# Blocked expert matmuls of a transformer layer pair: the loads of the down matrices issued by another engine

## What is computed

```python
def hierarchical_moe(h, rg_w, rg_b, re_w, re_b, w_gate, w_up, w_down):
    ...
    xs = xt[slot_tok].reshape(n_blocks, MOE_BLOCK, D)

    def expert_block(args):
        xb, e = args
        a = xb @ w_gate[e]
        u = xb @ w_up[e]
        return (jax.nn.silu(a) * u) @ w_down[e]

    ys = lax.map(expert_block, (xs, block_expert)).reshape(n_slots, D)
    ys = ys * slot_gate[:, None].astype(ys.dtype)
    out = jnp.zeros((T, D), ys.dtype).at[slot_tok].add(ys)
```

## Time and profile before

| | us |
|---|---|
| Median of 3 runs | 2011.5 |
| Lowest and highest | 2010.38, 2014.53 |
| The profiled execution's own time | 2010.09 |
| Its span, first to last instruction | 2008.8 |
| TensorE busy | 1814.8 |
| VectorE, ScalarE, GpSimd busy | 846.3, 437.2, 982.7 |
| Moved on q1 (SP), q10 (ScalarE), q0 (GpSimd) | 315.12, 19.46, 10.78 MB |

### The profile page before, as it was taken

The page is one execution under the profiler, slowest core; times in us unless marked ns, Lnnn a source line. Parts: engine busy times, 40 slices in busy tenths (PEclk is TensorE's granted clock), DMA queues, the critical chain, the costliest instruction groups (busy, mean ns, idle before and its releaser), DMA issues.

```text
span 2008.8 us, 27496 instructions
## 1 busy us (share of the span) xinstructions
PE 1814.8 (90%) x9716; PEld 1274.7 (63%) x9716; DVE 846.3 (42%) x1248; ACT 437.2 (22%) x813; POOL 982.7 (49%) x532
## 2 busy tenths in 40 slices
PE   8999999999999899999999889998968978969783
PEld 6888888887676678888888656765733333323231
DVE  6444433310444577444444489876341111111114
ACT  3111100100344432111100144552421111111112
POOL 6888887777444378888887533321211111101001
PEclk9999999999999999999999989999979989979887
DMA  4333372433111133333333212210588999999995
GB/s 160 94 96 102 106 267 88 145 94 94 53 57 50 43 89 91 101 95 94 94 112 100 73 53 73 66 54 28 235 312 325 401 403 399 401 415 412 411 393 207
DMA packets 56977, 346.00 MB, mean 172 GB/s; under 512 B 8474, under 2 KB 8858, under 8 KB 44896
## 3 DMA queue, kind: packets, MB, share of 16 engines
q1 hardware_dynamic: 44640, 315.12, 43.0%
q10 hardware_dynamic: 7968, 19.46, 2.6%
q0 software_dynamic: 4320, 10.78, 1.6%
HBM read 475.06 MB, written 19.66 MB: 246 GB/s over the span
## 4 chain that ended last, share of the span: by engine, by line
PE 71%; DMA 14%; DVE 10%; ACT 3%; issue 1%; POOL 1%; SPq 0%; DVEq 0%; ACTq 0%; POOLq 0%
PE bank L471 31%; PE bank L442 12%; DMA big<-w_up_in 11%; PE bank L1850 7%; PE bank L723 4%; PE bank L1349 4%; PE bank L1868 2%; DVE big L1075 2%; PE bank L490 2%; PE bank L1463 2%; DMA ring<-w_down_in 1%; PE bank L1876 1%; PE bank L641 1%; DVE state L1060 1%; PE bank L701 1%
## 5 line engine op out<-in xcount | busy, mean ns | idle before, releaser
L282 POOL TENSOR_TENSOR weights_hi_parts<-ring,ones 128x1024 fp32r<-128x1024 f32 (+1 forms) x174 | 351.4, 2019 | 291.9 <-PE bank L471 127.7
L284 POOL TENSOR_TENSOR ring_parts<-ring,weights_hi_parts 128x1024 fp32r<-128x1024 f32 (+1 forms) x174 | 468.7, 2693 | 13.6
L471 PE MATMUL bank<-attention_buffers_parts,weights_hi_parts 128*128 128x512 f32 x832 | 325.6, 391 | 11.4 <-DVE ring_parts L510 10.0
L471 PE MATMUL bank<-state_parts,weights_hi_parts 128*128 128x512 f32 x832 | 324.4, 390 | 0.0
L471 PE MATMUL bank<-attention_buffers_parts,ring_parts 128*128 128x512 f32 x832 | 324.2, 390 | 0.0
L1850 PE MATMUL bank<-big,work 128*32 128x512 f32 x1440 | 227.5, 674 | 51.3 <-DMA big<-w_up_in 51.1
L442 PE MATMUL bank<-big_parts,weights_hi_parts 128*128 128x512 f32 x704 | 216.8, 389 | 1.2 <-POOL ring_parts L284 1.2
L1950 POOL TENSOR_TENSOR small<-small 128x1 f32<-128x1 f32 x51 | 9.6, 189 | 375.0 <-DVE small L1773 375.0
L895 POOL TENSOR_TENSOR ring_parts<-ring,weights_hi_parts 128x1024 fp32r<-128x1024 f32 x32 | 80.6, 2520 | 222.6 <-ACT weights_hi_parts L892 222.6
L471 PEld LDWEIGHTS bank<-attention_buffers_parts,weights_hi_parts 128*128 128x128 f32 x832 | 156.6, 188 | 44.8 <-issue 10.5
L471 PEld LDWEIGHTS bank<-state_parts,weights_hi_parts 128*128 128x128 f32 x832 | 156.6, 188 | 33.0 <-issue 0.5
(11 more groups left out here) (391 smaller groups left out, 2833.6 us busy)
## 6 DMA issues: line engine op xcount, KB each, us to landing
big<-w_up_in SPq DMA_DIRECT2D x54, 2048.0 KB
ring<-wdense_in SPq DMA_DIRECT2D x176, 512.0 KB, 3.5
state<-w_down_in SPq DMA_DIRECT2D x37, 2048.0 KB
big<-w_gate_in SPq DMA_DIRECT2D x36, 2048.0 KB
attention_buffers<-w_gate_in SPq DMA_DIRECT2D x18, 2048.0 KB
ring<-w_down_in SPq DMA_DIRECT2D x18, 2048.0 KB
ring<-wff_in SPq DMA_DIRECT2D x32, 704.0 KB, 4.1
y_rows<-big ACTq DMA_DIRECT2D x1, 8192.0 KB, 28.0
```

The lines of the kernel that those rows point to most:

```text
L282: po.tensor_tensor(hi, raw, ones[:, 0:1].to_broadcast([128, words]), ALU.mult).then_inc(PO.sem, 1)
L284: po.tensor_tensor(lo, raw, hi.bitcast(F32), ALU.subtract) \
L471: m = pe.matmul(out, x, y_, start=j + n == 0, stop=j == len(pairs) - 1 and n == len(ts) - 1)
```

## The change

All down loads of the loop are issued by ScalarE, on its own queue. In ScalarE's loop `load_down` stands behind the silu and ahead of the stores of the previous block, and loads for block c + 2 while c is worked on. It waits for the same step of TensorE as before. SP's loop keeps the gate and up loads alone. The skipped load for block 2 is gone, and with it the 16 in the third set's wait. Ahead of its first block ScalarE waits for the tables.

```diff
-    def load_expert(m, b, e, needed=None):
+    def load_expert(m, b, e, needed=None, eng=sp):
 
         if needed is None:
-            d = sp.dma_start(sets[b][m], experts_d[m][e])
+            d = eng.dma_start(sets[b][m], experts_d[m][e])
         else:
-            d = sp.dma_start(sets[b][m], experts_d[m][bass.ds(e, 1), :, :].rearrange("a p c -> p (a c)"), cond=needed)
+            d = eng.dma_start(sets[b][m], experts_d[m][bass.ds(e, 1), :, :].rearrange("a p c -> p (a c)"), cond=needed)
         d.then_inc(s_wexp[m][b], 16)
...
-        pe.wait_ge(s_wexp[2][b], i * 16 + (16 * (c // SETS) + (32 if b == 2 else 16)))
+        pe.wait_ge(s_wexp[2][b], i * 16 + (16 * (c // SETS) + 16))
...
     def load_down(i, c):
 
-        e = sp.value_load(exp_i[0:1, bass.ds(i * SETS + c, 1)].bitcast(I32), min_val=0, max_val=N_EXP - 1)
-        needed = sp.value_load(need[0:1, bass.ds(i * SETS + c, 1)].bitcast(I32), min_val=0, max_val=1)
-        sp.wait_ge(PE.sem, at_step(PE, PE_D, i, c - SETS + 1))
-        load_expert(2, c % SETS, e, needed)
+        e = ac.value_load(exp_i[0:1, bass.ds(i * SETS + c, 1)].bitcast(I32), min_val=0, max_val=N_EXP - 1)
+        needed = ac.value_load(need[0:1, bass.ds(i * SETS + c, 1)].bitcast(I32), min_val=0, max_val=1)
+        ac.wait_ge(PE.sem, at_step(PE, PE_D, i, c - SETS + 1))
+        load_expert(2, c % SETS, e, needed, ac)
...
     with sp.Fori(0, laps["sp"]) as i:
         for c in range(SETS, 2 * SETS):
             load_first(i, c)
-            load_down(i, c - 1)
-    load_down(laps["sp"], SETS - 1)
...
+    ac.wait_ge(DV.sem, tables.base)
     act_copy(0, 0)
     act_silu(0, 0, 2)
     with ac.Fori(0, laps["ac"]) as i:
...
             act_copy(i, c)
             act_odd(i, c - 1)
             act_silu(i, c)
+            load_down(i, c + SETS - 1)
             act_store(i, c - 1)
```

## The result

| | before | changed |
|---|---|---|
| Median, us | 2012.15 (4 runs) | 2060.28 (4 runs) |
| Lowest and highest | 2010.38, 2014.53 | 2059.64, 2063.5 |
| The profiled execution, span | 2010.09, 2008.8 | 2060.82, 2059.6 |

The ratio is 1.0239, with a 95% interval of 1.0225 to 1.0254. The change costs 48.1 us; 55.8 were forecast, with a range of 2040 to 2084. A fourth run of the kernel before moved its median from 2011.5 to 2012.15.

The account below looks back on a forecast made before the run. The prediction took the DMA engines, busy share 1.00 over 413 us, to bound the block loop. Its terms, 9 + 30.8 + 5 + 11 = 55.8 us, gave a median of 2067 us from 2011.5, range 2040 to 2084.

Parts of the forecast that it names:

- Start of the loop: Loop start: down loads 3 and 4 share the engines with gate and up loads, delaying gate/up 5; cost 9 us.
- Four gaps: After up loads 14, 20, 26 and 38: engines idle through gate/up until the next gate load; 7.7 us each, 30.8.
- the one that I had called the weakest: In each burst of loads: all down loads overtake the burst's last up load; the gaps rest on it.
- one of the forecast's signs of being wrong: End of the loop: the forecast is wrong if block 50's down load still lands after its up load.
- Short gaps: Behind up loads 23, 29, 35, 47: ScalarE issues some 2 us later, engines wait; 5 us, between 0 and 8.
- The 31.6 in its upper bound: Four-gap share of the range's upper end: 10.5 + 31.6 + 8 + 11 + 10, 71 us above 2011.5.
- Order at the end: End of the loop: down loads 49 and 50 served ahead of up load 50, 11.0 us later; 5.5 if only one.
- Down waits: TensorE's waits for down matrices in the loop: 4.0 us go, but nothing is counted as gained.
- ScalarE: zero forecast: ScalarE between silu and next copy: some 1.9 us more work just fits in 3.32; zero cost, 10 us without cover.
- no change: Rival for the queues: ScalarE's gets engines only when SP's is empty, or bytes alone decide; 2011 us, chance 0.04.
- The half case: Rival for the bursts: one down load of each pair stays behind the up load; 20 us, 2032, chance 0.10.
- The bound on ScalarE: Rival in undisturbed blocks: issuing takes ScalarE 1 us or more, making copies late; 18 us on top, 2085, chance 0.08.

Follow-up runs that it names:

- the second profile of the changed kernel: The changed kernel run once more unaltered, on the chip of the two kernels that moved half of the down loads: 2059.0 us, ratio 1.0223.
- the two split kernels: Changed kernel with only part of the down loads on ScalarE, the rest on SP: buffer sets 0 and 1, 2035.9 us; set 2 alone, 2034.3 us.
- the one with 4 KB pieces: Changed kernel with the down matrices laid out in HBM so that down loads move in 4 KB pieces, not 16 KB: 2022.8 us, ratio 1.0065.
- the control: Kernel before, all loads on SP's queue, with down loads in 4 KB pieces: 2014.9 us, ratio 1.0014.
- the one with the swap on SP: Kernel before with the down load of block n-1 issued ahead of block n's gate and up loads on SP's queue: 2055.7 us, ratio 1.0233.
- the reads alone: Kernel before with ScalarE also reading each down load's two registers behind its silu, issuing no loads: 2014.6 us, ratio 1.0016.

## Why the prediction held, step by step

The direction, the mechanism and the range were right; the number was 7 us high. In part that is luck: the terms are all about the loop, which took 46.2 us more for 55.8 forecast, and 4.5 us ahead of the loop, in no term, made up for some of the miss. Gate/up 14, 20, 26, 38 and 50 start 16.1, 23.2, 29.6, 39.5 and 47.5 us later against the loop's start; about 19, 26, 35, 46 and 55 were forecast. By its terms, from the start times of gate/up 5, 50 and 53 counted from gate/up 0:

1. Start of the loop: 9 forecast. Gate/up 5 comes 54.8 us after gate/up 0 where it came after 46.5: 8.3.
2. Four gaps: 7.7 us each, 30.8, forecast. Measured from load to load 5.6, 7.9, 4.9 and 5.2: 23.6. This is the term that was mis-sized, and the step behind it is that all down loads of a burst overtake its last up load, the one that I had called the weakest. They nearly do. D14 is issued at 1601.40; counted from the loop's start (4.5 us late) and with the 8.3 of term 1 taken off, that is 1588.6, against 1586.30 in the earlier trace rows, 2.3 us later than SP did it. It is still moving when U14 lands at 1618.94: the last piece ends at 1620.3. D50 too ends after U50, 1996.6 against a landing at 1995.2. Read to the letter that is one of the forecast's signs of being wrong. It covers 0.1 to 2.0 us of each gap, and the gap opens all the same. What held D13 and D14 up stood ahead of them in their own queue. The first piece of D13 moves at 1598.3, 3.9 us after its issue, where D8's, with nothing else in flight, moves after 1.0. D14's moves at 1612.6, 2.8 us after D13's last. In both stretches (1594.4 to 1598.2, 1609.8 to 1612.6) ScalarE's queue moves only the small stores, whose pieces of 2 KB take turns with SP's of 16 KB:

```profile
q10 hardware_dynamic: 44, 0.05, 3.8%
...
q1 hardware_dynamic: 69, 1.10, 91.5%
q10 hardware_dynamic: 66, 0.09, 8.9%
```

Counted as above (12.8 us taken off), D13 is through at 1597 and D14 at 1607.5, where 1592 and 1603 were forecast, and U14 lands at 1606.1, not 1608.8. Gate/up also took 5.50, 5.47 and 5.09 us behind three of the four waits, 6.61 behind one, where I had taken 6.4 for all.
3. Short gaps: 5 forecast. From load to load, as in term 2, 2.4 behind U35 and 1.6 behind U47, none behind U23 and U29: 4.0. Term 2 of the prediction says that no gap comes behind U35 and U47, and term 3 counts one there; term 3 was right. The 31.6 in its upper bound is four gaps of 7.9, which no term works out.
4. Order at the end: 11 forecast. In all, gate/up 50 comes 47.5 us later against the loop's start (506.9 and 459.4). The measured terms 1 to 3 make 35.9, which leaves 11.6 for the order and for the rate, 400 against 405 GB/s per busy us. I can't part the two by a run.
5. Down waits: 4.0 us gone, none left, nothing gained by it, as forecast.
6. ScalarE: zero forecast. Its load comes 1.2 us after the silu's end and its next copy is late after a real load (4.15 us of idle time in place of 3.32, and the pair of stores takes 1.84 instead of 1.25), and TensorE waits 0.2 us for it in the whole loop:

```profile
1557.49 0.28 ACT L1887 ACTIVATE weights_hi<-bank 128x128 f32<-128x128 f32 x1 [0.41 <-PE bank L1876]
1559.00 0.39 ACTq L954 DMA_DIRECT2D state<-w_down_in  x1
1559.64 1.84 ACTq L1902 DMA_DIRECT2D y_rows<-ring  x2
1561.91 0.60 ACT L1882 ACTIVATE weights_hi<-bank 128x512 f32<-128x512 f32 x1 [4.15 <-PE bank L1768]
```

The free blocks still take 7.07 us (1543.32 to 1550.38 between gate/up 5 and 6). The stores land after 9.9 us in the middle and 30.9 at worst, where they took 6.8 and 8.6 and 11 to 20 were forecast, and inside the loop nobody waits for them.

A gain of 1.3 us in the tail (gate/up 50 takes 5.09 instead of 6.37) brings the loop to 46.2 us more. The further 4.5 ahead of it make up the 50.8 us of the profiled execution. They come again in the second profile of the changed kernel (4.3), so they belong to the kernel, as far as two profiles can tell.

Of the rivals, the queue that waits its turn ("no change") fell with the times. The half case is what the two split kernels come near, 2036 and 2034 for its 2032. The bound on ScalarE didn't come in the changed kernel, but in the one with 4 KB pieces it came in small. What the Trainium skill says in "DMA: Bandwidth & Descriptors", in the section on issuing engines not being separate DMA queues, held as far as it goes: the transfers interleave on the same engines. That a second issuer costs nothing doesn't follow from it: here the interleaving gave up an order and cost 46 us in the loop.

## What to carry to other kernels

Where DMA is the bound, one queue is also a schedule: whatever is issued last is what the engines move while the computing engine frees the next buffer. Before moving a load to another queue, ask what it will now be served ahead of, and what is left to move when the load that everybody waits for has landed. Ask also what stands ahead of it in the new queue: here small stores held the down loads of a burst up by some 3 us. If a load must share, its share of the engines can be set by the size of its pieces, at the price of more pieces on the queue of the issuing engine, which can hold that engine up.

## What was not expected of the hardware

- Issuing on a queue can hold the issuing engine. With 512 pieces of 4 KB to a load on ScalarE's queue, one pair of small stores behind them took 22 us to issue; with 128 pieces of 16 KB the slowest issue of a store took 1.27 and 1.80 us in the two profiles of the changed kernel. SP is held too: in the control, with the 4 KB pieces on its queue, its longest issue of a load took 7.98 us, against 0.51 in the kernel before.
- The start of the loop moves by several us with changes that lie behind it or on another engine. Gate/up 0 begins at 1483.90 in the kernel before and in the one with the swap on SP, at 1488.4 and 1488.2 in the two profiles of the changed kernel, and at 1485.0 to 1491.4 in the others. The granted clock between 1425 and 1450 us is 1.00 in the first two and in the changed kernel with 4 KB pieces, which begins its loop at 1485.0, and 0.86 in both profiles of the changed kernel. The two don't go strictly together: with the reads alone the clock is 0.93 and the loop begins at 1491.4, the latest of all. Of the kernel before and of the changed one:

```profile
1425.00:1450.00 25.00, 22.32 (x112) 18.57 (x110) 7.11 (x9) 9.85 (x20) 9.85 (x11) 1.00 0.73 310
```

```profile
1425.00:1450.00 25.00, 22.32 (x94) 18.12 (x93) 6.30 (x7) 11.29 (x21) 9.99 (x11) 0.86 0.79 337
```

The cause stays open. The control with 4 KB pieces, in which ScalarE's program is that of the kernel before, shows the same 0.86 and begins its loop at 1488.3, so ScalarE's work is not needed for it.
- The share of a queue followed the size of its pieces, as pieces that alternate one for one would have it: 155 to 149 pieces gave 2.24 to 2.07 MB with 16 KB on both queues, 257 to 257 gave 3.88 to 0.95 MB with 4 KB on the second, and the up loads' waits fell from 125.0 to 39.3 us.
